# Encoder layer on one core: a shorter search per bit, two matmuls instead of three for the sample's down tile, another order around the turned rows, and a final norm on two engines

## What is computed

```python
affinity = softmax(x2d @ w_router)                   # n x 16
gates, idx = top_k(affinity.T, 2 * n // 16)          # 256 prompt tokens or 64 sample tokens per expert
xe = x2d[idx]
h = silu(xe @ w_gate) * (xe @ w_up)                  # per expert, 1024 wide
ye = (h @ w_down) * gates[..., None]
moe = zeros_like(x2d).at[idx].add(ye)
y = layer_norm(2 ** 0.25 * x + moe, ln2_w, ln2_b)
```

## Time and profile before

| | us |
|---|---|
| median of 3 runs | 4047.64 |
| lowest and highest run | 4042.63, 4048.93 |
| the profiled execution, own time | 4044.12 |
| its span | 4042.4 |

### The profile page before, as it was taken

How to read it: one execution, slowest core, us unless ns; L and a number is a source line. 1 busy time by engine, 2 the same in 40 slices (tenths; PEclk the granted TensorE clock), 3 DMA queues, 4 the chain that set the end, 5 groups by cost and what they waited for, 6 DMA issues and landing times. The chain is left out here.

```text
span 4042.4 us, 52348 instructions
## 1 busy us (share of the span) xinstructions
PE 3605.0 (89%) x19644; PEld 3022.3 (75%) x19644; DVE 2257.6 (56%) x3777; ACT 1512.8 (37%) x1878; POOL 258.3 (6%) x160
## 2 busy tenths in 40 slices
PE   5999979969999999996999159999999999999980
PEld 4888868856777777774777149999988888888880
DVE  4444467766777777774554654444444444444438
ACT  2111144425666666664232023333333333333323
POOL 0000000000000000000111000000011000101105
PEclk9999989988999999998999569999999999999995
DMA  2121155663222012202332035555555554555535
GB/s 101 57 71 57 59 180 213 223 206 64 53 52 51 20 37 53 51 7 93 134 136 109 0 117 161 161 153 167 153 150 160 167 158 150 165 162 152 154 83 214
DMA packets 314700, 470.32 MB, mean 116 GB/s; under 512 B 79072, under 2 KB 215008, under 8 KB 311904
## 3 DMA queue, kind: packets, MB, share of 16 engines
q1 hardware_dynamic: 299936, 416.45, 32.8%
q0 software_dynamic: 14656, 52.44, 5.5%
HBM read 352.83 MB, written 116.00 MB: 116 GB/s over the span
## 5 line engine op out<-in xcount | busy, mean ns | idle before, releaser
L63 PE MATMUL psum<-xeT_hi,w_hi 128*128 128x320 f32 x2048 | 636.8, 311 | 15.3 <-ACT y L1856 14.2
L65 PE MATMUL psum<-xeT_hi,w_lo 128*128 128x320 f32 x2048 | 633.4, 309 | 0.0
L64 PE MATMUL psum<-xeT_lo,w_hi 128*128 128x320 f32 x2048 | 633.4, 309 | 0.0
L1905 DVE TENSOR_TENSOR w_lo<-w_raw,w_hi 128x2048 fp32r<-128x2048 f32 x192 | 431.3, 2287 | 247.4 <-ACT w_hi L1842 247.4
L1842 ACT ACTIVATE w_hi<-w_raw 128x2048 fp32r<-128x2048 f32 x192 | 356.9, 1906 | 344.6 <-PE psum L65 199.6
L1210 ACT ACTIVATE p_hi<-psum 128x1024 fp32r<-128x1024 f32 x272 | 279.1, 1026 | 359.7 <-PE psum L65 359.6
L1246 DVE TENSOR_REDUCE mx<-psum 128x1 f32<-128x1024 f32 x256 | 313.6, 1225 | 160.8 <-PE psum L1136 160.8
L63 PEld LDWEIGHTS psum<-xeT_hi,w_hi 128*128 128x128 f32 x2048 | 384.9, 188 | 22.2 <-issue 20.8
L64 PEld LDWEIGHTS psum<-xeT_lo,w_hi 128*128 128x128 f32 x2048 | 385.0, 188 | 0.0
L65 PEld LDWEIGHTS psum<-xeT_hi,w_lo 128*128 128x128 f32 x2048 | 385.0, 188 | 0.0
L1264 DVE TENSOR_TENSOR p_lo<-p_raw,p_hi 128x1024 fp32r<-128x1024 f32 x272 | 333.3, 1225 | 82.7 <-ACT p_raw L1212 79.3
(11 more groups left out here) (302 smaller groups left out, 6547.3 us busy)
## 6 DMA issues: line engine op xcount, KB each, us to landing
w_raw<-in_w_gate SPq DMA_DIRECT2D x64, 1024.0 KB, 5.0
w_raw<-in_w_up SPq DMA_DIRECT2D x64, 1024.0 KB, 5.9
w_raw<-in_w_down SPq DMA_DIRECT2D x64, 1024.0 KB, 5.3
rec<-rec SPq DMA_DIRECT2D x20, 768.0 KB, 3.6
recb<-rec SPq DMA_DIRECT2D x20, 768.0 KB, 5.1
xa<-in_x SPq DMA_DIRECT2D x20, 512.0 KB, 4.4
xb<-in_x SPq DMA_DIRECT2D x20, 512.0 KB, 6.0
xo<-in_x SPq DMA_DIRECT2D x20, 512.0 KB, 3.2
```

What stands on the lines that cost most here:

```text
L63: pe.matmul(out, a[0], b[0], start=first, stop=False)
L64: pe.matmul(out, a[0], b[1], start=False, stop=False)
L65: return pe.matmul(out, a[1], b[0], start=False, stop=last)
L1905: v.tensor_tensor(w_lo[n % 4][:], raw[n % 4][:], w_hi[n % 4][:].bitcast(F32), ALU.subtract).then_inc(s["lo_made"], 1)
```

## The change

The change has four parts.

1. **Search.** The affinities are first transposed by PE so that (tile, expert) is on partitions: `affT_p` is 128 x 256, `affT_s` 64 x 128. A comparison with a per-partition candidate counts at once through `accum_out`. PE then sums partitions with the same expert by two matmuls of one column, one per group (`same`, and `same_s`, which is weighted by 4 so that both groups meet the same bound, 256). The 30 bits are written out instead of looped, so bit values are constants. After the search the thresholds are spread and turned back by PE. `vals` moves to ACT, with two subtractions on POOL, beside the search.
2. **The sample's down tile.** `hT_hi` and `hT_lo` become one tile `hT`, in which the 64 sample rows' high parts and their rests stand side by side. One matmul with 128 rows gives both products, so f takes two matmuls (with `w_hi`, with `w_lo`) and not three. The 64 rows of rests come out on other partitions: ACT takes both (`y_part` and `y`), and DVE adds them (`add_halves`).
3. **Order around the turned rows.** New places in `TURNS`, banks 7 and 2 for turning (`T_BANK`), banks 4, 5, 6 and 0, 1, 3 for `y` (`Y_BANK`). PE's waits at the top of the body go: it waits for turned block k only before the first use of k, and for `y` tile by tile. ACT and DVE interleave chunks 0 and 1 with the turned blocks. The body of expert 0 is written out ahead of the loop.
4. **Final norm.** ACT sums (`Copy` with `accum_out`) and squares the centred tile (`Square` with `accum_out`), DVE applies everything in two `scalar_tensor_tensor`, SP issues loads and stores. POOL has nothing to do. All 20 tiles are written out, with eight load buffers and four store buffers.

```diff
+                pe.transpose(ps[:, 5, 0:P], aff[:, 0:P], c.ident)
+                pe.transpose(ps[:, 5, P:2 * P], aff[:, P:2 * P], c.ident)
+                pe.transpose(ps[0:NS, 6, 0:P], aff[:, 2 * P:NT * E], c.ident).then_inc(s["aff_turned"], 1)
+                for i in range(BITS):
+                    pe.wait_ge(s["compared"], i + 1)
+                    pe.matmul(ps[:, 0, 0:1], same[:], count[:, 0:1], start=True, stop=True)
+                    pe.matmul(ps[:, 0, 1:2], same_s[:], count[0:NS, 1:2], start=True, stop=True
+                              ).then_inc(s["counted"], 1)
...
+                for i in range(BITS):
+                    bit = 1 << (BITS - 1 - i)
+                    v.wait_ge(s["candidate"], i + 1)
+                    v.tensor_scalar(above_p[:], affT_p[:], cand[:, 0:1].bitcast(F32), None, ALU.is_ge, ALU.add,
+                                    accum_out=count[:, 0:1])
+                    v.tensor_scalar(above_s[:], affT_s[:], cand[0:NS, 1:2].bitcast(F32), None, ALU.is_ge, ALU.add,
+                                    accum_out=count[0:NS, 1:2]).then_inc(s["compared"], 1)
+                    v.wait_ge(s["counted"], i + 1)
+                    step(v.tensor_scalar(took[:], ps[:, 0, 0:2], float(CAP_P), float(bit), ALU.is_ge, ALU.mult))
...
-                            ins = mm3(pe, ps[:, bank0 + st, :], (hT[0][:, f, rows], hT[1][:, f, rows]),
-                                      (hi[:, f % 4, :], lo[:, f % 4, :]), f == 0, f == NF - 1)
+                            if st < 2:
+                                lo_rows = slice(LO + st * P, LO + st * P + n)
+                                ins = mm3(pe, ps[:, Y_BANK[half][st], :], (hT[:, f, rows], hT[:, f, lo_rows]),
+                                          (hi[:, f % 4, :], lo[:, f % 4, :]), f == 0, f == NF - 1)
+                            else:
+                                both = hT[:, f, CAP_P:LO]
+                                pe.matmul(ps[:, Y_BANK[half][st], :], both, hi[:, f % 4, :], start=f == 0, stop=False)
+                                ins = pe.matmul(ps[:, Y_BANK[half][st], :], both, lo[:, f % 4, :], start=False,
+                                                stop=f == NF - 1)
...
-    TURNS = [(0, 2), (0, 6), (1, 1), (1, 3), (1, 6), (2, 0), (2, 2), (2, 5)]
+    TURNS = [(0, 3), (0, 6), (1, 1), (1, 3), (1, 5), (1, 7), (2, 1), (2, 3)]
...
-                    pe.wait_ge(s["y_taken"], e * 6)
-                    pe.wait_ge(s["xT_lo_made"], e * DK + DK)
...
+                def add_up(t):
+                    a.wait_ge(x_in[t % R], 16 * (t // R + 1))
+                    a.activation(summing[t % 2][:], x[t % R][:], ACT.Copy, accum_out=at(total, t)
+                                 ).then_inc(s["summed"], 1)
...
+                    v.scalar_tensor_tensor(out=z[t % 2][:], in0=x[t % R][:], scalar=at(negmean, t), in1=ln_w[:],
+                                           op0=ALU.add, op1=ALU.mult).then_inc(s["weighted"], 1)
...
+                    v.scalar_tensor_tensor(out=o[t % S][:], in0=z[t % 2][:], scalar=at(rstd, t), in1=ln_b[:],
+                                           op0=ALU.mult, op1=ALU.add).then_inc(s["o_made"], 1)
```

More of the change, by code:

```diff
@@ L1553, in routing_phase @@
     G = 2 * E
+    NS = (NT - NTP) * E
     with ExitStack() as ph:
         sb = lambda n, s, dt=F32: ph.enter_context(nc.sbuf_tensor(n, s, dt))
[L1556 to L1559, removed]
+        thr, cand, took = (sb(n, [P, 2], I32) for n in ("thr", "cand", "took"))
+        affT_p, affT_s = sb("affT_p", [P, 2 * P]), sb("affT_s", [NS, P])
+        above_p, above_s = sb("above_p", [P, 2 * P]), sb("above_s", [NS, P])
+        count = sb("count", [P, 2])
+        same = sb("same", [P, P])
+        same_s = sb("same_s", [NS, P])
+        row = sb("same_row", [P, E])
+        thr_wide = sb("thr_wide", [E, 2, P], I32)
+        thr_row = sb("thr_row", [P, G])
+        full = sb("full", [P, G])
+        ones = sb("ones", [P, P])
         mask = sb("mask", [P, 2, NT, E])
@@ L1586, in _, with step @@
                 n = [0]
-                def step(ins, sem=placed):
+                def step(ins):
                     n[0] += 1
[L1591 to L1614, removed]
-                    search(v.tensor_tensor(took[:], ps[:, 0, 0:G], cap[:], ALU.is_ge))
-                    search(v.tensor_tensor(took[:], took[:], bit[:], ALU.mult))
-                    search(v.tensor_tensor(thr[:], thr[:], took[:], ALU.bitwise_or))
-                    search(v.tensor_scalar(bit[:], bit[:], 1, None, ALU.logical_shift_right))
-                    assert k[0] == STEPS
@@ L1698, in experts @@
         def experts(eng, body):
-            with eng.Fori(0, E - 1) as e:
+            body(0, True)
+            with eng.Fori(1, E - 1) as e:
                 body(e, True)
@@ L1804, in down @@
                     turns = list(range(DK)) if half == 1 and more else []
-                    bank0 = 4 if half == 0 else 0
                     for st, n in ST:
@@ L1850, in take_y @@
                     a.wait_ge(s["y_scored"], e * 6 + (3 * half + st + 1))
-                    bank = (4 if half == 0 else 0) + st
+                    bank = Y_BANK[half][st]
                     if half == 0 and st == 0:
@@ L2008, in final_norm_phase @@
         out_rows = d["out"].rearrange("(t p) n -> t p n", p=P)
-        def tiles(eng, *stages):
-            with eng.Fori(0, NT // R) as i:
-                for step in range(R + len(stages) - 1):
-                    for back, stage in enumerate(stages):
-                        if 0 <= step - back < R:
-                            stage(i, step - back, i * R + (step - back))
+        at = lambda tile, t: tile[:, t:t + 1]
         with nc.Block() as block:
@@ L2030, in _ @@
+                for b in range(S):
+                    sp.wait_ge(out[b], 16 * (NT // S))
             @block.scalar
             def _(a):
[L2032 to L2041 removed]
@@ L2085, in build @@
+                mean(0)
+                v.wait_ge(s["w_in"], 16)
+                for t in range(NT):
+                    if t + 1 < NT:
+                        mean(t + 1)
+                    weigh(t)
+                    if t >= 1:
+                        if t == 1:
+                            v.wait_ge(s["b_in"], 16)
+                        scale(t - 1)
+                        shift(t - 1)
+                scale(NT - 1)
+                shift(NT - 1)
 def build(nc, shapes, phases=99):
```

291 lines of the change are left out of this document (184 added, 107 removed).

## The result

The changed kernel takes **3900.4 us** (median of four runs, 3896.99 to 3902.54) where the kernel before took 4046.9 beside it: a ratio of 0.9637, 95% interval 0.9624 to 0.965. Forecast were 3917, with a range of 3894 to 3942, and "faster" with 0.98. The profiled execution took 3902.54 in all, its span is 3900.7. The direction and the range held. One term, the search, was 12.5 us too small, and one, the final norm, met its number with wrong steps behind it.

A forecast was written before the change was run, and what follows sets the result against it. PE's list was taken to bound the experts' stage, PE and DVE in turn the search, DVE the old norm. 26 + 2 + 58 + 17 + 1 + 32 less, 1.3 + 4.5 more: 130 less, 3917 us, range 3894 to 3942.

The forecast's parts named there:

- Search, 26 less: Search, 30 bits: a bit takes 2.81 us instead of 3.68, 84.3 instead of 110.3 in all.
- comparison and counting: Search bit on DVE: two accumulator instructions, 0.45 and 0.32, plus reads of 0.12 each, 1.01 us for 1.34.
- PE's answer: Search bit: two float32 products, four passes for two, 0.21 us per further pass, 1.15 in all.
- Three small steps: Search bit: bit taken, candidate and threshold remain, 0.65 us (0.5 to 0.7).
- Rival E: Parts gain more: search passes hide (2.4 us per bit), norm at 2.7 per tile; 3901 us, chance 0.13.
- Around the search, 2 less: `vals` leaves DVE, 4.3 us, against transposes and copies, 1.1, and the thresholds' way back, 1.3.
- Sample's tile, 58 less: Experts' down tile: 16 matmuls of 0.2267 us fewer per expert, 3.63 each, times 16 experts.
- Top of the body, 17 less: Experts: PE's 1.13 us lost waiting for ACT's last `y` goes, 15 times.
- First turned block, 4.5 more: Experts: PE reaches the first turn just ahead of the third gather; priced 0.3 us per expert, 0 to 15 in all.
- Final norm, 32 less: Final norm: 66.4 us instead of 97.8, first tile 11.3, 19 more 55.1; store issued 0.6 sooner.
- A to D: Gather/chunks hold PE, 3942, 0.08; norm passes half rate, 3959, 0.05; search hardly gains, 3932, 0.10; slower than before, 0.01.
- B: Final norm: the two DVE passes run at half rate, 2.35 us each, norm 42 more; 3959 us, chance 0.05.

The follow-up runs named there:

- before_unrolled: The kernel before, with the search's 30 bits written out on PE and DVE instead of looped: 4034.8 us against 4046.7, ratio 0.9972.
- third_matmul: The changed kernel with the sample's down tile issuing its second matmul once more, three per value of f: 3956.3 us.
- waits_back: The changed kernel with PE's two waits at the top of the body put back: 3947.2 us, 47 slower.
- mean_on_act: The changed kernel with ACT's sum scaled by -1/D, so DVE has no mean step in the norm: 3899.1 us.
- third_z: The changed kernel with three buffers for z in the final norm instead of two, DVE's mean step kept: 3897.6 us.
- short_wait: The changed kernel with PE's top-of-body waits back, but ACT taking the last tile's new rows first, so the stop is shorter: 3922.6 us.

## Why the prediction was right, and where it wasn't

- **Search, 26 less: mis-sized.** It saved 30 x 1.285 = 38.5. By its three pieces: *comparison and counting*, 1.01 forecast, 0.73 measured (2234.52 to 2235.25). The two reads of 0.12 were added in full; they take 0.08 and 0.07, and neither adds to the time, since one runs beside the next comparison and the other inside its own. The forms cost 0.40 from start to start and 0.33, near the middle of the bounds. *PE's answer*, 1.15 forecast, 1.20 measured; 0.21 per further pass was right, it is 0.22 to 0.25. *Three small steps*, 0.65 forecast, 0.47 measured: they were taken from steps of 32 columns (0.19, 0.23 apart) but have 2 columns (0.16, 0.20 apart), and the threshold's update costs only 0.08, since the next comparison waits for the candidate alone. The branch was 0.52 in the forecast and 0.49 in `before_unrolled`. Rival E named 2.4 us per bit, but for hidden passes; those are not hidden. The Trainium skill says that an operation with an accumulator output is two instructions (VectorE: DVE Perf Modes, "Two Vector instructions with no wait between them"); the rows agree, DVE_READ_ACCUMULATOR being the second, and it is nearly free here.
- **Around the search, 2 less: about right.** `vals` 4.1 less (4.3 forecast). The first comparison starts 2.28 behind the last softmax step's start, 2.05 before: 0.2 more instead of 1.1, since the transposes and copies run beside DVE's setting up. What is left of the stretch's 36.8 besides the 30 bits and this is 1.5 more for the thresholds' way back (1.3 forecast). Together 2.4 less.
- **Sample's tile, 58 less:** right, 3.64 per expert in `third_matmul`. The end 1.3 more: right, 12.51 from PE's last start to the norm's first load, 11.19 before.
- **Top of the body, 17 less, and the first expert 1 earlier:** a little small. The distance of 96.63 falls by 4.89; less 3.64 this leaves 1.25 per expert, 19, against 1.13. The stop ahead of the first expert (1.14) is gone too, but two more groups of three matmuls then start 0.80 apart, at half the granted clock, and not 0.44, which gives 0.6 back. What the prediction didn't see is what the new order *prevents*: with the two-pass tile the old waits would have cost 47 (`waits_back`), since their stop would have grown to 1.84 and the clock fell behind eight of them.
- **First turned block, 4.5 more:** right in kind, 1 to 3 in size; in this profile the gather is late in four experts by up to 0.8, not in all by 0.3.
- **Final norm, 32 less: right in sum, wrong in its steps.** The first tile's way took 14.9, not 11.3: ACT's third sum, placed ahead of the first root, waits for a load behind the weights' and bias's. The other 19 tiles took 53.5, not 55.1, and behind the last pass 3.1 instead of 5.7 pass, 2.6 less where 0.6 was forecast. And "the largest counts, 2.9", the DMA engines' term, named the wrong engine: DVE sets 2.84 by its two passes, the reciprocal between them and the wait for its own `z`, in which the mean step disappears (`mean_on_act`, `third_z`). The estimate of 360 GB/s at a full share was no limit: a share of 1.02 goes with 418. The sign named for it, a share near 1, came all the same (0.99). That the numbers met was luck.
- **Rivals.** A to D didn't come; of E both halves came in part, a bit of 2.4 us without the hidden passes and a norm tile of 2.84 for 2.7. For B: both passes take 1.28 for 1024 columns with float32 sources in SBUF, 1.20 to 1.21 from start to start. The Trainium skill (Vector Engine (DVE) Microarchitecture Reference, "Points that are easy to get wrong") says that the scalar-tensor-tensor form with two such sources halves its throughput; that doesn't hold here.

The error was 16.6 us between medians. By the stretches the search accounts for 12.5 of it, the experts for 2.6, and what stands around the search for nearly nothing (0.7 better than forecast in its own stretch, 0.8 worse in the next); the remainder of 1.5 is within the scatter.

## What to carry to other kernels

In a chain where two engines answer each other, price each step by a row of its own width and by what the next step really waits for; an instruction that nobody waits for costs only its issue. Before adding work ahead of a wait, ask what the wait will become: here a stop that grew from 1.15 to 1.84 us cost more than twice its growth, because the clock fell behind eight of 15. When a sum fits, still check its parts: the norm's 32 us were right and their reason wasn't. And a DMA share near 1 is no proof of a bound; take time from another engine and see whether the rate rises.

## What the runs showed of the hardware that was not expected

- The granted clock: stops of PE of 1.15 us in a list without other gaps left it at 1.00 in all 15 bodies (`short_wait`); behind eight of 15 stops of 1.84 it fell to half for 3.4 us (`waits_back`). Why the others were spared is open.
- The DMA engines' busy share stood at 0.99 for 361 GB/s and at 1.02 for 418 GB/s with the same kinds of transfer.
- DVE's read of its accumulator takes 0.08 us and starts together with the next instruction; ACT's takes 0.19, and the next instruction starts 0.09 to 0.10 behind it.
- A wait of DVE on its own last instruction costs 0.19 us between two passes of 1024 columns (1.39 instead of 1.20) and shows as no idle time.
